# Per-head normalisation of queries and keys in block 2: one VectorE operation a head in place of a VectorE and a GpSimd pass

## The chip, the cores and the metric

The kernel runs on one core of a Trainium2 chip, with the engines TensorE, VectorE, ScalarE, GpSimd and the DMA queues beside one another. The metric is the device time of one execution in microseconds. Before the change it is 2656.02 us, the median of 3 runs (2654.87 to 2657.49).

## What is computed

Two transformer blocks behind one another on a sequence of 256 tokens and a width of 1024, each with two layers. The second, in which the change lies, carries 256 latent and 256 context tokens. In each of its layers one projection feeds a convolution branch, a neighbourhood attention and a grouped-query attention. The change touches how the last one's queries (8 heads) and keys (2 heads), 64 columns each, are normalised and rotated:

```python
def rmsnorm_2(x, g):
    xf = x.astype(jnp.float32)
    y = xf * lax.rsqrt(jnp.mean(xf * xf, axis=-1, keepdims=True) + EPS)
    return (y * g.astype(jnp.float32)).astype(x.dtype)

g_kc = rmsnorm_2(heads(gkc, GQA_KV_HEADS), k_norm_g[l])
q = axial_rope(rmsnorm_2(heads(gq, GQA_Q_HEADS), q_norm_g[l]), pos_row, pos_col)
k = axial_rope(rmsnorm_2(heads(gk, GQA_KV_HEADS), k_norm_g[l]), pos_row, pos_col)
cq = rmsnorm_2(heads(gqc, GQA_Q_HEADS), q_norm_g[l])
```

Latent tokens are normalised and rotated, context tokens only normalised. In the last layer the context has no queries of its own, only keys.

## The kernel before

Each engine has its own instruction stream, written out by hand, and they meet through semaphores. Block 2's projection stage is a row of items, each the products of one piece of weights (1024 rows by 256 columns) with the activations: four `glu` items (convolution branch), then `gkv`, `gq` (2), `nak` (2), `naq` (2) and `nav` (2), which are items 4 to 12. Products are done in three terms from an upper and a lower part of the float32 values: ScalarE copies the upper part of a piece (L1155), VectorE subtracts it and leaves the lower part (L773, `split2_low`), and TensorE takes both (L1913 with the activations as the moving side, L1948 with the weights moving). "Split n" below is L773 on piece n, and TensorE waits for it before item n. Item 11 is the first `nav` item, at L1948.

What VectorE does in this stage stands in the table `LEAD`, one list for each layer: numbers are taps of the depthwise convolution (L3235, 31 taps on 4 chunks, each 512 columns in layer 0 and 256 in layer 1), `(LOW, n)` is split n, `(SUMS, s)` and `(NORMS, 0)` belong to the normalisation. The stretch around the change is

```python
# layer 0
(SUMS, 3), 5, (LOW, 10), 7, (NORMS, 0), (LOW, 11), 8, (LOW, 12), 7, (LOW, 13), 9, (LOW, 14), 3
# layer 1
(SUMS, 3), 11, (LOW, 10), 11, (NORMS, 0), 2, (LOW, 11), 4, (LOW, 12), 12, (LOW, 13), 8, (LOW, 14)
```

The normalisation works on `gtok`, 128 tokens on the partitions by 4 token tiles `s` (0 and 1 latent, 2 and 3 context) by 640 columns (10 heads of 64; heads 8 and 9 are the keys). In profiles `gtok` lies in the buffer `G`, the factors `gss` in `small`, the rotation's temporaries in `A`. ScalarE squares (L1639), VectorE sums each head (L3255), ScalarE takes the root (L1664), VectorE the reciprocal (L3264), and in `g_norms` VectorE multiplies each tile by its factors, one operation for a tile (L3269), which counts `g_normed`.

GpSimd waits for `g_normed` of tile s. At s = 0 it first issues four DMAs that load two tables of the neighbourhood attention's bias (L1052). Then it multiplies the tile by the norm's weights, the 8 query heads (L1062) and the 2 key heads (L1065), and for the latent tiles it rotates: four products (L987), a difference (L989) and a sum (L990), which counts `roped_g`. Context tiles count it behind the multiplication. After the four tiles it adds the mask to the two tables (L1086). TensorE transposes `gtok` (L2440) when `roped_g` is complete, behind the projection's last item; then come the convolution branch's mean (L2432, which wants all taps) and the attention pairs (L2459, with the softmax's steps on VectorE L2876, L2880) woven with the products of the gates.

Of the kernel before, what the change touches and what calls it, by code (L numbers as in the profile page):

```python
# [16 lines left out]
ALU = mybir.AluOpType  # L17
# [3 lines left out]
P = 128  # L21
# [27 lines left out]
HD = 64  # L49
# [340 lines left out]
def program(nc, g, out):  # L390

    with ExitStack() as ctx:
# [29 lines left out]
        gain_qk = sb("gain_qk", DEPTH * 2 * HD)[:, :].rearrange("p (l k d) -> p l k d", l=DEPTH, k=2)  # L422
# [116 lines left out]
        gtok = G[:, 0:2560].rearrange("p (s n) -> p s n", s=4)  # L539
# [23 lines left out]
        gss = take(40).rearrange("p (s h) -> p s h", s=4)  # L563
# [22 lines left out]
        def pcol(name, i=0, layer=None, per=0):  # L586
# [54 lines left out]
        gsq_ready, gss_ready, groot_ready, g_normed, roped_g = (sem(n) for n in (  # L641
            "gsq_ready", "gss_ready", "groot_ready", "g_normed", "roped_g"))
# [291 lines left out]
        def _(pool):  # L934
# [57 lines left out]
            for l in range(DEPTH):  # L992
                chain = Chain(pool, pool_done, l * POOL_CHAIN1)
# [11 lines left out]
                for s in range(2):  # L1005
                    v = idxt[:, s, 0:576].rearrange("p (h d) -> p h d", h=9)
# [8 lines left out]
                for s in range(2):  # L1015
                    if s:
                        pool.wait_ge(roped_qk, (l * 2 + 1))
                    v = qkv[:, s, 0:2048].rearrange("p (h d) -> p h d", h=16)
# [14 lines left out]
            chain = Chain(pool, pool_done, (DEPTH * POOL_CHAIN1))  # L1033
            item, masked, bias_n, used = ITEM2, 0, 0, 0
            for layer in range(DEPTH):
                last = layer == DEPTH - 1
# [15 lines left out]
                        pool.dma_start(dst, src).then_inc(bias_landed[n % 2], 16)  # L1052

                for s in range(4):
                    h0 = 8 if last and s >= 2 else 0
                    pool.wait_ge(g_normed, 4 * layer + s + 1)
                    if s == 0:
                        load_bias(0)
                        load_bias(1)
                    v = gtok[:, s, :].rearrange("p (h d) -> p h d", h=10)  # L1060
                    if not h0:
                        chain(pool.tensor_tensor(v[:, 0:8, :], v[:, 0:8, :],  # L1062
                                                 gain_qk[:, layer, 0, :].unsqueeze(1).broadcast_to([P, 8, HD]),
                                                 ALU.mult))
                    ins = pool.tensor_tensor(v[:, 8:10, :], v[:, 8:10, :],  # L1065
                                             gain_qk[:, layer, 1, :].unsqueeze(1).broadcast_to([P, 2, HD]), ALU.mult)
                    if s >= 2:
                        ins.then_inc(roped_g, 1)
                        continue
                    chain(ins)  # L1070
                    chain.settle()
                    v = gtok[:, s, :].rearrange("p (h r e f) -> p h r e f", h=10, r=2, e=2)
                    cs_, sn_ = [t[:, s].unsqueeze(1).broadcast_to([P, 10, 2, 16]) for t in (cos2, sin2)]

                    pool.wait_ge(gss_ready, 4 * (layer + 1))
                    if s:
                        pool.wait_ge(roped_g, 4 * layer + 1)
                    rotate(v[:, :, :, 0, :], v[:, :, :, 1, :], cs_, sn_, [rope2[:, n] for n in range(4)], chain,
                           roped_g)
# [1437 lines left out]
        def _(dve):  # L2517
# [393 lines left out]
            for l in range(DEPTH):  # L2911
                items, poss, norm = l * ITEMS1, l * PIECES1, l * 3
                chain = Chain(dve, dve_done, (DVE_START) + l * DVE_CHAIN1)
# [90 lines left out]
                def head_rows(t):  # L3004
# [10 lines left out]
                                         op1=ALU.mult).then_inc(adt_ready, 1)  # L3015
# [11 lines left out]
                for u in range(8):  # L3027
                    s = u // 4
                    dve.wait_ge(relu_ready, (l * 8 + (u + 1)))
                    for e in range(2):  # L3030
                        h, n = 2 * (u % 4) + e, 2 * u + e
                        if h:
                            dve.wait_ge(score_step, (steps + n))
                        dve.scalar_tensor_tensor(out=score[s], in0=relu_buf[:, u % 2, T * e:T * e + KEYS[s]],
                                                 scalar=wi[:, s, h:h + 1],
                                                 in1=score[s] if h else caus[:, s, 0:KEYS[s]], op0=ALU.mult,
                                                 op1=ALU.add).then_inc(score_step, 1)
# [54 lines left out]
                for i in range(PAIRS + 2):  # L3092
                    if 1 <= i < PAIRS + 1:
                        c = i - 1
                        dve.wait_ge(decay_ready, done + c + 1)
                        for e in range(2):
                            h, half = 2 * c + e, mt[c % 2][:, e, :]
                            dve.scalar_tensor_tensor(out=half[:, 0:T], in0=half[:, 0:T], scalar=dt[:, 0, h:h + 1],
                                                     in1=cbm[:, h // 8, 0, :], op0=ALU.mult, op1=ALU.mult)
                            ins = dve.scalar_tensor_tensor(out=half[:, T:384], in0=half[:, T:384],  # L3100
                                                           scalar=dt[:, 1, h:h + 1], in1=cbm[:, h // 8, 1, 128:T],
                                                           op0=ALU.mult, op1=ALU.mult)
                        ins.then_inc(mt_ready, 1)
                    qkv_ahead("head", 2 * i - 1)
                    if i < PAIRS:
# [3 lines left out]
                        for e in range(2):  # L3109
                            h, half, row = 2 * i + e, mt[i % 2][:, e, :], M[(i + 1) % 2][:, T * e:T * (e + 1)]  # L3110
# [77 lines left out]
            for layer in range(DEPTH):  # L3188
# [70 lines left out]
                def g_norms():  # L3259

                    for s in range(4):
                        h0 = 8 if last and s >= 2 else 0
                        dve.wait_ge(groot_ready, 4 * layer + s + 1)
                        chain(dve.reciprocal(gss[:, s, h0:10], gss[:, s, h0:10]))  # L3264
                    chain.settle()
                    for s in range(4):
                        h0 = 8 if last and s >= 2 else 0
                        v = gtok[:, s, HD * h0:640].rearrange("p (h d) -> p h d", d=HD)
                        dve.tensor_tensor(v, v, gss[:, s, h0:10].unsqueeze(2).broadcast_to([P, 10 - h0, HD]), ALU.mult)\  # L3269
                           .then_inc(g_normed, 1)  # L3270

                n_issued = 0
                for n in range(4):
# [211 lines left out]
```

## Time and profile before

| | |
|---|---|
| median of 3 runs | 2656.02 us |
| the profiled execution | 2657.64 us, its span 2655.80 us |
| TensorE busy (products) | 2617.2 us, 99% |
| VectorE busy | 1928.6 us, 73% |
| ScalarE busy | 1278.2 us, 48% |
| GpSimd busy | 594.0 us, 22% |
| mean granted TensorE clock | 0.997 |

Shares of busy time are averages over stages. The stages of the change lie at 1380 to 1460 us (layer 0) and 2195 to 2270 us (layer 1). In the views, PE is TensorE, PEld its weight load, DVE VectorE, ACT ScalarE, POOL GpSimd; L12 is line 12 of the kernel.

### The profile page before, as it was taken

The numbers are of one execution on the slowest core, as the hardware profiler recorded it, in microseconds if no ns is written. First come the engines' busy times: TensorE is split into PE (matmuls) and PEld (weight loads), VectorE is DVE, ScalarE is ACT, GpSimd is POOL, SyncE is SP. The second block draws the span as 40 slices with busy tenths as digits, with TensorE's granted clock in tenths as the row PEclk, the third lists the DMA queues.
The fourth block names the chain that finished last, engine by engine and source line by source line (L and its number), as shares of the span: only waits on it lengthen the run. The fifth ranks groups of instructions, "written<-read, shape, count | busy, mean of one in ns | idle before, by whom it ended". The sixth has DMA issues, their size and how long they took to land.

```text
span 2655.8 us, 40458 instructions
## 1 busy us (share of the span) xinstructions
PE 2617.2 (99%) x17054; PEld 2285.5 (86%) x17054; DVE 1928.6 (73%) x2550; ACT 1278.2 (48%) x1659; POOL 594.0 (22%) x419
## 2 busy tenths in 40 slices
PE   8999999999999999999999999999999999999999
PEld 7889888888889987988898777778888899889887
DVE  7867576885876657687799655468778779865884
ACT  5445546544444545544523544544444443655543
POOL 3411010331330001132105301024303203411430
PEclk9999999999999999999999999999999999999999
DMA  7555795555555688455333322245555544434653
GB/s 245 186 192 179 245 301 165 185 186 194 190 181 177 206 269 270 159 190 194 91 96 100 85 70 64 70 142 192 188 186 191 181 120 129 122 116 147 219 182 103
DMA packets 442330, 445.57 MB, mean 168 GB/s; under 512 B 13711, under 2 KB 433672, under 8 KB 442150
## 3 DMA queue, kind: packets, MB, share of 16 engines
q1 hardware_dynamic: 438744, 436.80, 51.5%
q0 software_dynamic: 2400, 5.40, 1.0%
q8 instruction: 135, 2.21, 0.4%
q10 hardware_dynamic: 1006, 0.79, 0.1%
q14 instruction: 45, 0.37, 0.0%
HBM read 441.79 MB, written 1.17 MB: 167 GB/s over the span
## 4 chain that ended last, share of the span: by engine, by line
PE 90%; DVE 4%; issue 2%; ACT 2%; DMA 1%; POOL 1%; SPq 0%; ACTq 0%; DVEq 0%; POOLq 0%
PE bank L1953 31%; PE bank L1913 22%; PE bank L1957 16%; PE bank L1905 6%; PE bank L1948 4%; PE bank L2229 2%; PE bank L2468 1%; PE bank L2459 1%; PE bank L2139 1%; DVE lower L773 1%; DVE R L3235 1%; PE bank L2312 1%; DMA ring<-in_w_in 0%; PE bank L2326 0%; DMA bias_na<-rpb_scratch 0%
## 5 line engine op out<-in xcount | busy, mean ns | idle before, releaser
L1226 ACT ACTIVATE upper<-ring 128x2048 fp32r<-128x2048 f32 (+1 forms) x238 | 443.9, 1867 | 625.8 <-PE bank L1957 618.8
L2616 DVE TENSOR_TENSOR lower<-ring,upper 128x2048 fp32r<-128x2048 f32 (+1 forms) x238 | 596.0, 2505 | 190.2 <-ACT upper L1226 189.9
L1953 PE MATMUL bank<-h_pair,upper 128*128 128x512 f32 x2464 | 606.5, 393 | 10.8 <-DVE h_pair L2633 5.9
L1953 PEld LDWEIGHTS bank<-h_pair,upper 128*128 128x128 f32 x2464 | 455.8, 189 | 102.0 <-issue 11.7
L1957 PE MATMUL bank<-h_pair,lower 128*128 128x256 f32 x2464 | 339.7, 284 | 0.0
L1913 PE MATMUL bank<-h_up,lower 128*128 128x512 f32 (+1 forms) x1280 | 337.5, 346 | 0.7 <-DVE h_low L2683 0.7
L1957 PEld LDWEIGHTS bank<-h_pair,lower 128*128 128x128 f32 x2464 | 325.6, 192 | 11.4
L1953 PE MATMUL bank<-hid_pair,upper 128*128 128x512 f32 x1232 | 297.4, 392 | 0.0
L980 POOL TENSOR_TENSOR A<-A 128x512 f32<-128x512 f32 x77 | 209.4, 2719 | 334.5 <-ACT A L1275 334.5
L1913 PEld LDWEIGHTS bank<-h_up,lower 128*128 128x128 f32 x1280 | 223.6, 189 | 46.3 <-issue 17.3
L1953 PEld LDWEIGHTS bank<-hid_pair,upper 128*128 128x128 f32 x1232 | 225.7, 188 | 43.2
L773 DVE TENSOR_TENSOR lower<-ring,lower 128x2048 fp32r<-128x2048 f32 x70 | 164.9, 2356 | 99.9 <-ACT lower L1155 99.9
L766 DVE TENSOR_TENSOR lower<-ring,upper 128x2048 fp32r<-128x2048 f32 (+1 forms) x66 | 149.7, 2268 | 105.1 <-ACT upper L1147 105.1
L1913 PE MATMUL bank<-h_low,lower 128*128 128x512 f32 (+1 forms) x640 | 218.7, 342 | 0.0
L1155 ACT ACTIVATE lower<-ring 128x2048 fp32r<-128x2048 f32 x70 | 134.4, 1920 | 113.1 <-DMA ring<-in_w_in 82.5
L978 POOL TENSOR_TENSOR A<-A 128x512 f32<-128x512 f32 x77 | 121.3, 1575 | 277.6 <-DVE A L2724 146.5
L1905 PE MATMUL bank<-upper,h_pair 128*128 128x256 f32 x896 | 168.9, 290 | 0.0
L1957 PEld LDWEIGHTS bank<-hid_pair,lower 128*128 128x128 f32 x1232 | 159.8, 191 | 7.1
L1957 PE MATMUL bank<-hid_pair,lower 128*128 128x256 f32 x1232 | 162.0, 283 | 0.0
L3235 DVE SCALAR_TENSOR_TENSOR R<-R,params 128x512 f32<-128x512 f32 (+1 forms) x240 | 153.6, 706 | 0.5
L1905 PEld LDWEIGHTS bank<-upper,h_pair 128*128 128x128 f32 x896 | 140.5, 192 | 9.0 <-issue 7.7
L1147 ACT ACTIVATE upper<-ring 128x2048 fp32r<-128x2048 f32 (+1 forms) x66 | 124.2, 1881 | 46.9 <-PE bank L1913 28.0
(377 smaller groups left out, 4291.6 us busy)
## 6 DMA issues: line engine op xcount, KB each, us to landing
ring<-in_w_ffn_in SPq DMA_DIRECT2D x154, 1024.0 KB, 5.1
ring<-in_w_ffn_out SPq DMA_DIRECT2D x56, 1024.0 KB, 4.9
ring<-in_w_mix_in SPq DMA_DIRECT2D x48, 1024.0 KB, 5.4
ring<-in_w_mod SPq DMA_DIRECT2D x48, 1024.0 KB, 7.4
ring<-in_w_in SPq DMA_DIRECT2D x42, 1024.0 KB, 5.3
ring<-in_w_ffn_out SPq DMA_DIRECT2D x28, 768.0 KB, 4.2
ring<-in_w_mix_out SPq DMA_DIRECT2D x16, 1024.0 KB, 5.5
ring<-in_w_in SPq DMA_DIRECT2D x16, 512.0 KB, 4.6
```

The source lines that it names most:

```text
L766: eng.tensor_tensor(lowers[piece.slot][:, 0:w], slots[piece.slot][:, 0:w], uppers1[piece.up][:, 0:w].bitcast(F32), ALU.subtract).then_inc( ...
L773: eng.tensor_tensor(lowers[piece.slot], slots[piece.slot], uppers2[piece.up].bitcast(F32), ALU.subtract)\
L980: pool.tensor_tensor(buf, buf, r, ALU.mult).then_inc(glu_scaled, 1)
L1147: act.activation(uppers1[piece.up][:, 0:w], slots[piece.slot][:, 0:w], ACT.Copy).then_inc(up1_ready, 1)
L1155: act.activation(uppers2[piece.up], slots[piece.slot], ACT.Copy).then_inc(up2_ready, 1)
L1226: act.activation(f.upper(p)[:, 0:n], slot[:, 0:n], ACT.Copy).then_inc(up_ready, 1)
L1905: mm = pe.matmul(o, x_[:, k, tokens], w_[:, c], start=k == 0 and n == 0, stop=k == KD - 1 and n == 2)
L1913: mm = pe.matmul(out, w_[:, w_cols], x_, start=first and n == 0, stop=last and n == 2)
L1953: pe.matmul(bank[:, 0:2 * T], up[:, cols], x_pair.rearrange("p e t -> p (e t)"), start=first, stop=False)
L1957: return pe.matmul(bank[:, 0:T], low[:, cols], x_pair[:, 0, :], start=False, stop=last)
L2616: dve.tensor_tensor(f.lower(p)[:, 0:n], slot[:, 0:n], f.upper(p)[:, 0:n].bitcast(F32), ALU.subtract)\
L3235: ins = dve.scalar_tensor_tensor(out=dst, in0=src, scalar=w, in1=dst, op0=ALU.mult, op1=ALU.add)
```

## The change

VectorE's four multiplications by tile and GpSimd's multiplications by the weights are replaced by one scalar_tensor_tensor on VectorE for each head: the head's 64 columns times its factor (a column of `gss`, one value for each partition) times the weights `gain_qk`. That is 40 operations in layer 0 and 24 in layer 1 (10, 10, 2 and 2). `g_normed` is counted by the last head of a tile. GpSimd keeps the table DMAs, the rotation of the latent tiles and the masks; for context tiles it only passes the count on.

```diff
@@ -1052,23 +1052,13 @@
                         pool.dma_start(dst, src).then_inc(bias_landed[n % 2], 16)
 
                 for s in range(4):
-                    h0 = 8 if last and s >= 2 else 0
                     pool.wait_ge(g_normed, 4 * layer + s + 1)
                     if s == 0:
                         load_bias(0)
                         load_bias(1)
-                    v = gtok[:, s, :].rearrange("p (h d) -> p h d", h=10)
-                    if not h0:
-                        chain(pool.tensor_tensor(v[:, 0:8, :], v[:, 0:8, :],
-                                                 gain_qk[:, layer, 0, :].unsqueeze(1).broadcast_to([P, 8, HD]),
-                                                 ALU.mult))
-                    ins = pool.tensor_tensor(v[:, 8:10, :], v[:, 8:10, :],
-                                             gain_qk[:, layer, 1, :].unsqueeze(1).broadcast_to([P, 2, HD]), ALU.mult)
                     if s >= 2:
-                        ins.then_inc(roped_g, 1)
+                        pool.sem_inc(roped_g, 1)
                         continue
-                    chain(ins)
-                    chain.settle()
                     v = gtok[:, s, :].rearrange("p (h r e f) -> p h r e f", h=10, r=2, e=2)
                     cs_, sn_ = [t[:, s].unsqueeze(1).broadcast_to([P, 10, 2, 16]) for t in (cos2, sin2)]
 
@@ -3265,9 +3255,11 @@
                     chain.settle()
                     for s in range(4):
                         h0 = 8 if last and s >= 2 else 0
-                        v = gtok[:, s, HD * h0:640].rearrange("p (h d) -> p h d", d=HD)
-                        dve.tensor_tensor(v, v, gss[:, s, h0:10].unsqueeze(2).broadcast_to([P, 10 - h0, HD]), ALU.mult)\
-                           .then_inc(g_normed, 1)
+                        for h in range(h0, 10):
+                            v = gtok[:, s, HD * h:HD * (h + 1)]
+                            ins = dve.scalar_tensor_tensor(out=v, in0=v, scalar=gss[:, s, h:h + 1],
+                                                           in1=gain_qk[:, layer, h // 8, :], op0=ALU.mult, op1=ALU.mult)
+                        ins.then_inc(g_normed, 1)
 
                 n_issued = 0
                 for n in range(4):
```

## Rows read from the trace of the kernel before

**Rows 1.** the page: busy time by engine, and the chain by engine

```profile
PE 2617.2 (99%) x17054; PEld 2285.5 (86%) x17054; DVE 1928.6 (73%) x2550; ACT 1278.2 (48%) x1659; POOL 594.0 (22%) x419
...
PE 90%; DVE 4%; issue 2%; ACT 2%; DMA 1%; POOL 1%; SPq 0%; ACTq 0%; DVEq 0%; POOLq 0%
```

**Rows 2.** TensorE's waits (waiter <- releaser: total us, times, longest)

```profile
PE bank L1913 <- DVE R L3306: 2.5, 1, 2.5
PE bank L1948 <- DVE lower L773: 2.0, 1, 2.0
PE bank L1948 <- DVE R L2825: 1.7, 1, 1.7
...
PE bank L2440 <- ACT sq L1696: 0.6, 1, 0.6
```

**Rows 3.** the chain, layer 1 (start us, us, what)

```profile
2204.19 3.56 DVE R L3235 x9
...
2240.15 24.81 PE bank L1948 x192
...
2267.05 1.73 PE bank L2432 x8
```

**Rows 4.** windows (us: engines' busy time, PEclk the granted clock)

```profile
2228.50:2240.10 11.60, 9.67 (x81) 9.46 (x79) 11.57 (x24) 6.32 (x11) 3.83 (x5) 1.00 0.64 197
2240.10:2243.80 3.70, 3.65 (x18) 3.65 (x19) 3.70 (x4) 0.05 (x1) 3.53 (x4) 0.54 0.91 285
...
2178.00:2186.00 8.00, 6.33 (x54) 6.16 (x53) 7.37 (x15) 3.81 (x5) 0.00 (x0) 1.00 0.51 162
...
2318.50:2322.60 4.10, 3.88 (x20) 3.91 (x21) 3.23 (x9) 3.04 (x5) 1.26 (x2) 0.58 0.71 196
```

**Rows 5.** VectorE's groups from 2195 to 2236 us (busy us, mean ns)

```profile
L3235 DVE SCALAR_TENSOR_TENSOR R<-R,params 128x256 f32<-128x256 f32 x70 | 28.3, 478 | 0.0
```

**Rows 6.** timeline of VectorE, layer 1 (start us, us, what)

```profile
2235.13 1.97 DVE L3269 TENSOR_TENSOR G<-G,small 128x640 f32<-128x640 f32 x4
2237.01 0.88 DVE L3235 SCALAR_TENSOR_TENSOR R<-R,params 128x256 f32<-128x256 f32 x2
2237.81 2.29 DVE L773 TENSOR_TENSOR lower<-ring,lower 128x2048 fp32r<-128x2048 f32 x1
...
2244.09 2.97 DVE L773 TENSOR_TENSOR lower<-ring,lower 128x2048 fp32r<-128x2048 f32 x1
2246.98 11.93 DVE L3235 SCALAR_TENSOR_TENSOR R<-R,params 128x256 f32<-128x256 f32 x12
```

**Rows 7.** timeline of GpSimd, layer 1 ([idle before <- releaser])

```profile
2236.26 2.47 POOL L1052 DMA_DIRECT2D bias_na<-rpb_scratch  x4 [79.80 <-DVE G L3269]
...
2252.04 3.94 POOL L987 TENSOR_TENSOR A<-G,trig 128x320 f32<-128x320 f32 x4 [0.17 <-POOL G L1065]
...
2270.92 2.61 POOL L1052 DMA_DIRECT2D bias_na<-rpb_scratch  x4 [8.06 <-DVE A L2880]
```

**Rows 8.** timeline of VectorE in block 1, the nearest short operation

```profile
1029.75 0.34 DVE L3100 SCALAR_TENSOR_TENSOR A<-A,small,R 128x128 f32<-128x128 f32 x1
1030.01 0.48 DVE L3111 TENSOR_SCALAR A<-bank,small 128x256 f32<-128x256 f32 x1
```

**Rows 9.** timeline of VectorE, layer 0

```profile
1411.94 3.03 DVE L3269 TENSOR_TENSOR G<-G,small 128x640 f32<-128x640 f32 x4
1414.89 4.16 DVE L773 TENSOR_TENSOR lower<-ring,lower 128x2048 fp32r<-128x2048 f32 x1
```

**Rows 10.** the chain, layer 0

```profile
1428.83 23.03 PE bank L1948 x192
```

**Rows 11.** timeline of GpSimd, layer 0

```profile
1413.06 2.51 POOL L1052 DMA_DIRECT2D bias_na<-rpb_scratch  x4 [110.66 <-DVE G L3269]
1415.59 1.30 POOL L1062 TENSOR_TENSOR G<-G,gain_qk 128x512 f32<-128x512 f32 x1
```

**Rows 12.** timeline of VectorE in block 1, GpSimd rotating beside it

```profile
359.54 0.81 DVE L3100 SCALAR_TENSOR_TENSOR A<-A,small,R 128x128 f32<-128x128 f32 x1
```

## Prediction, made before the changed kernel was run

> **What bounds the kernel now.** I read the shares of the page first [rows 1]: TensorE is busy 99% of the span, and its products are 90% of the chain that ended last. So work added to VectorE, or taken off GpSimd, moves the end only where TensorE waits for one of them. The list of TensorE's waits [rows 2] has one such wait beside the change: 2.0 us at L1948 for `lower`, VectorE's output of L773. The chain through layer 1's projection stage [rows 3] shows its place: up to 2240 us it consists of VectorE's own instructions, and at 2240.15 TensorE resumes, right behind weight split 11. The normalisation of the queries and keys stands ahead of split 11 in VectorE's order, so every microsecond added to it is a microsecond for TensorE. In layer 0 the same order has room: split 11 is written at 1419.05 (1414.89 + 4.16) [rows 9] and its first product is due at 1428.83 [rows 10], 9.8 us later.
>
> The wait in layer 1 has a second price. The granted clock was 1.00 before it and 0.54 from 2240.1 to 2243.8 [rows 4], so TensorE ran there mostly at 1.2 GHz. The same 192 products took 24.81 us [rows 3] against 23.03 in layer 0 [rows 10]: 1.78 us.
>
> **VectorE and GpSimd at the same time.** A tap of 256 columns takes 0.478 us with GpSimd idle [rows 5]. Twelve taps behind one another took 11.93 us while GpSimd multiplied [rows 6], about 1.02 each, with one GpSimd product of 128x320 to each tap (four of them took 3.94 us from 2252.04) [rows 7]. A tap's columns are 256/0.96 = 0.27 us of this, so a GpSimd product holds VectorE off for 0.75; I take 0.76. The two engines take turns, one instruction each, however long either is: an operation of 128 columns took 0.81 us beside GpSimd [rows 12] and 0.34 alone [rows 8]. What counts is how many VectorE instructions are still to come when GpSimd begins.
>
> **The change, part by part.**
>
> *VectorE's four multiplications* (L3269) go. In layer 1 they took 1.88 us from the first start to the next instruction (2235.13 to 2237.01) [rows 6], in layer 0 2.95 us (1411.94 to 1414.89) [rows 9].
>
> *VectorE's per-head operations* come: 10+10+2+2 = 24 in layer 1, 40 in layer 0, each on 64 columns with a per-partition factor. The trace has none so short of this form. The nearest row is the form on 128 columns, whose successor starts 0.26 us later (1029.75 to 1030.01) [rows 8]; 64 columns less, at one per 1/0.96 ns, take off 0.067: 0.196 us. From below: the four TENSOR_TENSORs of 640 columns repeat every 0.74 us [rows 9], 0.07 over their columns, so 0.134 is the least for 64. From above, without overlap of neighbours, 0.28. I take 0.196, the value of the same form: 24 x 0.196 = 4.70 us in layer 1 (3.2 to 6.7), 40 x 0.196 = 7.84 in layer 0.
>
> The Trainium skill ("VectorE: DVE Perf Modes", the TRN2 errata section) speaks against this change: VectorE pays a fixed cost per instruction, so many small tiles pay it each time, and its figure from SBUF is 58 cycles plus the columns. By that, an estimate, 64 columns take 122 cycles, 0.127 us. The direction is that of the rows; the size is not, since for 128 columns the figure gives 0.19 where the row has 0.26.
>
> *GpSimd's 14 gain multiplications* (L1062, L1065) go. Its order becomes: four table DMAs, two rotations of six products each, then the mask additions. The table DMAs took VectorE no time in layer 1: its taps beside them began 0.40 us apart [rows 6, 7].
>
> *Layer 1, split 11.* The tenth operation ends at 2235.13 + 9 x 0.196 + 0.28 = 2237.17. GpSimd's first DMA follows 0.3 us behind (before, 2235.13 + 0.83 to 2236.26), the four take 2.47, and the first product comes 0.17 later for its semaphores [rows 7]: 2240.1. VectorE is through its 24 operations at 2239.83, so the first of the two taps goes ahead, to 2240.30. Then they take turns: GpSimd to 2241.06, second tap (0.27) to 2241.33, GpSimd to 2242.09, split 11 (2048 columns, 2.13) to 2244.2. Before, it was 2240.10. **Plus 4.1 us**: 2.8 of instructions, 1.3 of turns that GpSimd took behind the split before.
>
> *Layer 0, split 11.* GpSimd starts rotating at 1411.94 + 1.76 + 0.28 + 0.3 + 2.51 + 0.17 = 1416.95 [rows 9, 11]; 25 of the 40 operations are issued by then. Beside operations of 64 columns its twelve products come every 0.76 + 0.07 = 0.83 us: 10.0 us and some 0.5 of gaps between its groups, to 1427.5. VectorE gets one operation into each turn and one into each gap, 15 in all, so its 40th ends at 1427.5 too. Split 11 takes 2.2 more: 1429.8. TensorE wants it at 1428.83. **Plus 1.0 us**; of the 9.8 us of cover nothing is left. Bounds: nothing (at 0.134 the operations are done at 1417.3) and 2.5 us (two more turns).
>
> *What follows.* Layer 1: TensorE reaches the products of split 12 half of 24.8 us after 2244.2, at 2256.6; that split was ready at 2247.06 and is now some 4 us later [rows 6]. The taps' end hardly moves, since the turns of 14 multiplications are gone by then, and stays ahead of the mean's products at 2267.05 + 4 [rows 3]. Layer 0: eight taps of 0.66 (512/0.96 + 0.13), two mask additions and split 12 end at 1438.5, wanted at 1440.3. So the time freed on GpSimd pays VectorE back, but behind the instruction that TensorE waits for. An earlier rotation buys nothing: the transposes L2440 waited 0.6 us for ScalarE, not for GpSimd [rows 2].
>
> *The clock.* The low stretch of layer 1 stays (bounds: 1.78 us given back, if it falls where TensorE idles, and 1.78 more). The waits of 2.0 and 2.5 us were each followed by one, the 1.7 at L1948 was not (granted clock 1.00 from 2178 to 2186) [rows 2, 4]; the 1.0 of layer 0 should be without. The three runs spread by 2.6 us, one and a half such stretches, so some runs may escape the present one; with 6 us of wait none should. I add 0.3.
>
> **Sum.** 4.1 + 1.0 + 0.3 = 5.4 us. The profiled run took 2657.64 (span 2655.80), 1.6 above the median; the addition is the same for either: 2656.02 + 5.4 = 2661.4 us.
>
> **The rivals.**
> - *Forecast*, chance 0.50: both stages lose. 2661.4, own range 2660.0 to 2663.5.
> - *GpSimd gets in first*, 0.18. Split 11 of layer 0 took 4.16 us, 1.87 over its 2.29 [rows 6, 9], and was held from about 1415.0 although GpSimd's product was only issued at 1415.59 [rows 11]. If a rotation likewise holds VectorE during the last DMA of layer 1, each VectorE instruction caught behind it costs 0.8: three +2.5. About 2663.5. Against: the rotation stands behind a semaphore wait, that multiplication did not.
> - *Layer 0 stays covered*, 0.12: VectorE slips two short operations into a turn. The 40 are done by 1424, split 11 before 1428.83. Only layer 1 pays: 2660.4. Against: the 128-column operation, one to a turn [rows 12].
> - *Short operations cost 0.134*, 0.06: layer 0 nothing; in layer 1 they end at 2238.35, the split is issued at 2239.15, ahead of GpSimd's product, and ends at 2241.35. +1.25 and the 0.3: 2657.6. The skill's figure from the errata section leads to the same case.
> - *The low stretch falls into the wait*, 0.07: 1.78 back, 2659.6.
> - *The other side, no loss*, 0.07: GpSimd, free some 5 us earlier, shortens layer 1's pair stage, so that the 2.5 us wait at L3306 and the low stretch behind it (0.58) [rows 2, 4] go: 5.4 less 4.3, 2657.1. It decides if GpSimd is what that stage waits for. Against: it stood idle 8.06 us for VectorE before its next table DMA [rows 7].
>
> **How the numbers follow.** The range reaches from 2658.3 (layer 1 alone, its low stretch given back) to 2666.5 (three instructions caught, a second low stretch, some of layer 0's upper bound). 0.2% (5.3 us) is about what a measurement here can tell from none, and the forecast lies on that bound. Slower takes 0.6 of the forecast's chance, all of the second case and a little of the others: 0.50. Within 0.2%: 0.47. Faster, by a low stretch fewer elsewhere: 0.03.
>
> **What would show it.** Per-head operations 0.196 us apart while GpSimd is idle, 0.83 while it rotates. TensorE's wait at L1948 for L773 twice: 6 us in layer 1, 1 in layer 0. The taps of 2246 to 2262 with fewer at 1.02 us and more at 0.4, their end in place. GpSimd's busy time down by some 20 us. The prediction falls if layer 0 shows no wait, if split 11 of layer 1 ends before 2243, or if a low stretch comes or goes elsewhere.

## The result, and the profile after

The changed kernel takes 2667.14 us, the median of 4 runs (2665.52 to 2668.56), against 2655.44 for the kernel before in 4 runs beside it: ratio 1.0044, 95% interval 1.0032 to 1.0056, all of it above 0.2%. That is 11.7 us more where 5.4 were forecast, and 0.6 us above the upper end of the range. The profiled run took 2667.55 us with a span of 2665.7, 9.9 more than the span of before; the profiled run of the kernel before lies 2.2 us above the median of its four runs and this one 0.4, which is the rest of the 11.7.

The lines of the changed kernel lie 9 or 10 lower: the taps are L3225, the per-head operations L3260, the item with the weights moving is L1938 (before L1948), the first with the activations moving L1903 (before L1913), the masks are L1076. L773, L987, L989, L990 and L1052 are as before.

The page of the changed kernel, busy time by engine and the chain by engine:

```profile
PE 2618.6 (98%) x17054; PEld 2286.7 (86%) x17054; DVE 1932.6 (72%) x2606; ACT 1278.5 (48%) x1659; POOL 572.9 (21%) x405
...
PE 85%; DVE 9%; issue 2%; ACT 2%; DMA 1%; POOL 0%; SPq 0%; ACTq 0%; POOLq 0%
```

Against [rows 1], GpSimd works 21.1 us less and VectorE only 4.0 us more in the sum, yet VectorE's share of the chain went from 4% to 9%. The list of TensorE's waits (total us, times, longest) says where:

```profile
PE bank L1938 <- DVE lower L773: 12.3, 2, 9.4
```

Against the single wait of 2.0 us in [rows 2] there are now two, 2.95 us in layer 0 and 9.37 in layer 1. The chain of the changed kernel shows both (start us, us, what), first layer 1, then layer 0:

```profile
2233.42 4.36 DVE R L3225 x11
...
2238.10 9.37 DVE G L3260 x24
2247.47 0.79 DVE R L3225 x2
2248.26 2.21 DVE lower L773
...
2250.52 19.59 PE bank L1938 x148
```

```profile
1424.40 5.15 DVE G L3260 x12
1429.55 2.21 DVE lower L773
...
1431.80 13.26 PE bank L1938 x97
```

Between the reciprocals and split 11 there are now 9.30 us of per-head operations (2238.10 to 2247.40) in place of 1.88 [rows 6], and in layer 0 they are on the chain too.

The starts of TensorE's 17054 products, set against those of before one by one, give the account of the time. In layer 0 they are 3.1 us late behind the wait and 4.5 to 5.0 us late shortly after it, since the granted clock falls there. At 2181 us 1.5 us come back: the 1.67 us wait that stands there before [rows 2] is 0.3 in this run. In layer 1 another 7.4 are lost (10.4 late), at 2310 us 0.7 come back, and the end is 9.9 us late. So nearly all of it lies at the two waits. The windows of the changed kernel around them (us: busy time, then the granted clock):

```profile
1425.00:1431.50 6.50, 3.86 (x18) 2.85 (x16) 6.50 (x13) 1.33 (x3) 4.79 (x5) 1.00 0.17 49
1431.50:1434.90 3.40, 3.10 (x14) 3.10 (x15) 3.40 (x5) 0.66 (x1) 1.98 (x2) 0.50 0.61 214
...
2243.90:2254.00 10.10, 3.48 (x16) 3.48 (x17) 10.10 (x11) 1.91 (x1) 9.79 (x8) 0.50 0.30 92
```

TensorE worked at 1.2 GHz (granted clock 0.50) for 3.4 us behind the new wait of layer 0. In layer 1 the low stretch is longer than before [rows 4], but for the most part it lies in the wait itself: TensorE is busy for 3.48 us of it.

The ledger of VectorE in layer 1 closes to a few hundredths. Single operations on its timeline (start us, us):

```profile
2241.83 0.97 DVE L3260 SCALAR_TENSOR_TENSOR G<-G,small,gain_qk 128x64 f32<-128x64 f32 x1
2242.72 2.81 DVE L3260 SCALAR_TENSOR_TENSOR G<-G,small,gain_qk 128x64 f32<-128x64 f32 x1
2245.45 0.95 DVE L3260 SCALAR_TENSOR_TENSOR G<-G,small,gain_qk 128x64 f32<-128x64 f32 x1
2246.33 0.27 DVE L3260 SCALAR_TENSOR_TENSOR G<-G,small,gain_qk 128x64 f32<-128x64 f32 x1
2246.52 0.95 DVE L3260 SCALAR_TENSOR_TENSOR G<-G,small,gain_qk 128x64 f32<-128x64 f32 x1
```

and GpSimd's timeline beside them:

```profile
2240.45 2.47 POOL L1052 DMA_DIRECT2D bias_na<-rpb_scratch  x4 [79.51 <-DVE G L3260]
2242.93 0.88 POOL L987 TENSOR_TENSOR A<-G,trig 128x320 f32<-128x320 f32 x1
2243.75 0.87 POOL L987 TENSOR_TENSOR A<-G,trig 128x320 f32<-128x320 f32 x1
2244.57 0.86 POOL L987 TENSOR_TENSOR A<-G,trig 128x320 f32<-128x320 f32 x1
2245.40 0.92 POOL L987 TENSOR_TENSOR A<-G,trig 128x320 f32<-128x320 f32 x1
2246.40 0.99 POOL L989 TENSOR_TENSOR G<-A 128x320 f32<-128x320 f32 x1
2247.36 3.83 POOL L990 TENSOR_TENSOR G<-A 128x320 f32<-128x320 f32 x1
```

An operation beside an idle GpSimd lasts 0.28 us, and the next one starts 0.196 later. Twenty of the 24 are such. The operation of 2241.83 is held by 0.69 us while the third and fourth table DMA are issued. The one of 2242.72 is held by 2.53 us, through three of GpSimd's products, which follow one another without a gap. Two more are held by 0.67 us each, one product apiece. Together: 24 x 0.196 + 0.69 + 2.53 + 0.67 + 0.67 = 9.26 of the 9.30 us. Then it turns round: two taps and split 11 run unhindered (0.87 and 2.28 us) while GpSimd's sum of 2247.36 stands for 3.83 us. The wait follows: 2.0 as before, plus 4.70 - 1.88 = 2.8 for the longer instructions, plus 4.6 for the four holds, is 9.4.

In layer 0 the same two holds stand at the same place, 0.69 us at 1415.71 and 2.61 us at 1416.62 (an operation of 2.89), and nine operations behind them are held by one product each (0.97 to 0.99 us in place of 0.28). That is 7.84 + 0.69 + 2.61 + 9 x 0.70 = 17.4 of the 17.49 us from 1411.98 to 1429.47.

### The profile page after: what moved, and what is told of

Read it like the earlier page. It is cut to its first block, busy times and chain, and to the rows that moved or that the text cites. A ratio compares the mean times of both kernels' runs of the same rounds, so it can differ in the third digit from the quotient of the medians.

```text
span 2665.7 us, 40503 instructions
## 1 busy us (share of the span) xinstructions
PE 2618.6 (98%) x17054; PEld 2286.7 (86%) x17054; DVE 1932.6 (72%) x2606; ACT 1278.5 (48%) x1659; POOL 572.9 (21%) x405
## 4 chain that ended last, share of the span: by engine, by line
PE 85%; DVE 9%; issue 2%; ACT 2%; DMA 1%; POOL 0%; SPq 0%; ACTq 0%; POOLq 0%
PE bank L1943 31%; PE bank L1903 20%; PE bank L1947 16%; PE bank L1895 6%; DVE R L3225 3%; PE bank L1938 2%; DVE lower L773 2%; PE bank L2219 2%; PE bank L2458 1%; PE bank L2449 1%; PE bank L2129 1%; DVE G L3260 1%; PE bank L2302 1%; ACT lower L1145 1%; PE bank L2316 0%
## 5 line engine op out<-in xcount | busy, mean ns | idle before, releaser
L1903 PE MATMUL bank<-h_up,lower 128*128 128x512 f32 (+1 forms) x1280 | 337.4, 346 | 0.7 <-DVE h_low L2673 0.7
L1903 PEld LDWEIGHTS bank<-h_up,lower 128*128 128x128 f32 x1280 | 223.6, 189 | 46.2 <-issue 17.3
L773 DVE TENSOR_TENSOR lower<-ring,lower 128x2048 fp32r<-128x2048 f32 x70 | 163.8, 2340 | 101.1 <-ACT lower L1145 101.1
L1903 PE MATMUL bank<-h_low,lower 128*128 128x512 f32 (+1 forms) x640 | 218.7, 342 | 0.0
L3225 DVE SCALAR_TENSOR_TENSOR R<-R,params 128x512 f32<-128x512 f32 (+1 forms) x240 | 136.9, 642 | 0.5
```

The lines of the kernel that those rows point to most:

```text
L773: eng.tensor_tensor(lowers[piece.slot], slots[piece.slot], uppers2[piece.up].bitcast(F32), ALU.subtract)\
L1903: mm = pe.matmul(out, w_[:, w_cols], x_, start=first and n == 0, stop=last and n == 2)
L3225: ins = dve.scalar_tensor_tensor(out=dst, in0=src, scalar=w, in1=dst, op0=ALU.mult, op1=ALU.add)
```

## The experiments

Two theories stood after the comparison. By the first, *the holds beside GpSimd* make the loss: ahead of split 11 stand many short VectorE instructions, GpSimd's products hold them for some 0.7 us each, and the products right behind the table DMAs get in early and for three in a row. By the rival, the loss is the *number and duration of the instructions* themselves, or comes from what the change does on GpSimd, the rotation moved forward and the time freed.

**All tiles first.** GpSimd issues its table DMAs and then waits for all four tiles, so that no product stands beside a per-head operation.

```diff
 # GpSimd, changed kernel
                     if s == 0:
                         load_bias(0)
                         load_bias(1)
+                        pool.wait_ge(g_normed, 4 * layer + 4)
```

> The changed kernel, but GpSimd, after its four table DMAs, waits for all four tiles before it rotates the first. Theory 'holds' (the per-head operations cost 0.196 us as in the changed kernel's first ten; the rest of their 9.30 and 17.49 us was GpSimd's rotation holding the shared interface, from its last DMAs on): 24 operations in 4.7 us and 40 in 7.9, no TensorE wait at item 11 of layer 0, in layer 1 a wait of 5.5 to 7.5 us, since the two taps and split 11 now meet the rotation. About 2661. Theory 'the DMAs themselves hold it': operations beside the third and fourth DMA still take 0.7 us or more longer. Theory 'short operations slow down in a row': 9 and 17 us as in the changed kernel, and its 2667.

Measured: 2658.55 us (10 runs) against 2655.26 (25 runs), ratio 1.0012 (1.0003 to 1.0021). VectorE's timeline of this kernel, layer 0 and then layer 1, and GpSimd's in layer 1:

```profile
1411.28 7.95 DVE L3261 SCALAR_TENSOR_TENSOR G<-G,small,gain_qk 128x64 f32<-128x64 f32 x40
...
2233.08 4.79 DVE L3261 SCALAR_TENSOR_TENSOR G<-G,small,gain_qk 128x64 f32<-128x64 f32 x24
2237.78 0.87 DVE L3226 SCALAR_TENSOR_TENSOR R<-R,params 128x256 f32<-128x256 f32 x2
2238.57 2.28 DVE L773 TENSOR_TENSOR lower<-ring,lower 128x2048 fp32r<-128x2048 f32 x1
```

```profile
2235.42 2.47 POOL L1052 DMA_DIRECT2D bias_na<-rpb_scratch  x4 [81.08 <-DVE G L3261]
2237.94 6.70 POOL L987 TENSOR_TENSOR A<-G,trig 128x320 f32<-128x320 f32 x4
```

With this wait the kernel is 3.3 us above the kernel before, and without it 11.7, each against its own runs of the kernel before: it takes back 8.4 us. The operations take 4.70 and 7.85 us, the predicted 0.196 each. Layer 0 has no wait any more, and the one in layer 1 is 4.7: the old 2.0 and the 2.8 of instructions. So the holds, with the low clock behind them, cost some 8.4 us and the instructions themselves the rest. The time expected was 2661 and the wait in layer 1 5.5 to 7.5 us, because the two taps and split 11 were to meet the rotation. They met it and weren't held: they took 0.87 and 2.28 us, and it was GpSimd's first product that lasted through all three (3.64 us of the 6.70 for four). The last two table DMAs (to 2237.89) stand beside the last operations here and hold nothing, where in the changed kernel one was held by 0.69 us. What differs is the product behind them, which must wait for the other tiles here and was ready there.

**The wait in layer 0 only**, to see whether the two layers add up.

```diff
                         load_bias(1)
+                        if layer == 0:
+                            pool.wait_ge(g_normed, 4 * layer + 4)
```

> The changed kernel with the wait for all four tiles in layer 0 only. By the account of the trace layer 0 costs 3.1 us of wait and 1.4 of low clock, layer 1 7.4: the wait at item 11 of layer 0 goes, and the time is 4.5 us under the changed kernel's 2667.1: 2662.6. If the losses were not additive (the later state of the ring of weights gives some back), 2664 to 2667.

Measured: 2663.36 us (5 runs) against 2655.33 (14 runs), ratio 1.0033 (1.0020 to 1.0046). Against the changed kernel's 2667.14 layer 0 gives back 3.8 us, where the trace had 4.5; the run with both waits gives back 4.8 more for layer 1, where the trace had 4.6 of holds. The wait in layer 1 is 9.6 us in this kernel and 9.4 without any edit, so layer 1's loss doesn't hang on layer 0's. No run has the wait in layer 1 alone.

**Only VectorE's part.** GpSimd keeps its 14 multiplications, so the weights are applied twice.

```diff
 # the kernel before, VectorE alone changed
-                        dve.tensor_tensor(v, v, gss[:, s, h0:10]... , ALU.mult).then_inc(g_normed, 1)
+                        for h in range(h0, 10):
+                            ins = dve.scalar_tensor_tensor(out=v, in0=v, scalar=gss[:, s, h:h + 1],
+                                                           in1=gain_qk[:, layer, h // 8, :], ...)
+                        ins.then_inc(g_normed, 1)
```

> Only VectorE's part of the change: per-head operations by factor and weights, while GpSimd keeps its 14 gain multiplications (the weights are thus applied twice). Theory: the loss sits in the operations caught beside GpSimd's products right behind its table DMAs, whatever these products are; wait in layer 1 9 us, in layer 0 3 us or more, since there are eight products more and the one of 512 columns is longer: 2667 to 2670. Rival, that it is the rotations moved forward that hold VectorE: without them 5 us less, 2660 to 2662.

Measured: 2672.52 us (4 runs) against 2655.33 (14 runs), ratio 1.0067 (1.0051 to 1.0084), 17.2 us more. TensorE's waits and VectorE's timeline, layer 0 and layer 1:

```profile
PE bank L1948 <- DVE lower L773: 15.4, 2, 8.7
```

```profile
1411.46 21.26 DVE L3270 SCALAR_TENSOR_TENSOR G<-G,small,gain_qk 128x64 f32<-128x64 f32 x40
...
2244.35 8.61 DVE L3270 SCALAR_TENSOR_TENSOR G<-G,small,gain_qk 128x64 f32<-128x64 f32 x24
2252.88 0.87 DVE L3235 SCALAR_TENSOR_TENSOR R<-R,params 128x256 f32<-128x256 f32 x2
```

The direction was foreseen, the size was not: 2.5 us above the end of what was expected, and it is layer 0, where the wait is 6.6 us and not 3. There GpSimd has 16 products for its first two tiles and four more for the others, and VectorE's 40 operations last (to 1432.7) until those 16 are over. In layer 1 the 24 operations take 8.6 us with a gain multiplication behind the table DMAs as they take 9.3 with a rotation there. So it isn't the rotation moved forward that holds VectorE, and that part of the rival is out. Its other part, the duration of the instructions, is the 3.3 us that the run with the wait for all tiles still costs.

**Only GpSimd's part.** Its 14 multiplications are left out, VectorE keeps its four; the weights are applied nowhere.

```diff
 # the kernel before, GpSimd alone changed
-                    if not h0:
-                        chain(pool.tensor_tensor(v[:, 0:8, :], ... gain_qk[:, layer, 0, :] ...))
-                    ins = pool.tensor_tensor(v[:, 8:10, :], ... gain_qk[:, layer, 1, :] ...)
                     if s >= 2:
-                        ins.then_inc(roped_g, 1)
+                        pool.sem_inc(roped_g, 1)
                         continue
```

> Only GpSimd's part of the change: its 14 gain multiplications are left out, VectorE keeps its four multiplications by the factors (the weights of queries and keys are thus applied nowhere). Theory: what was lost comes from VectorE's many instructions ahead of split 11; with four of them as before, split 11 begins ahead of GpSimd's first rotation product in layer 1 and the 2.0 us wait stays as it is, layer 0 keeps its cover: 2655 us, as the kernel before, within 1. Rival: the products that stand right behind the table DMAs hold VectorE wherever they are, and with rotations in place of gain multiplications there the wait grows: 2657 to 2659. If the freed time of GpSimd is worth something, 2653 or less.

Measured: 2654.36 us (10 runs) against 2655.33 (14 runs), ratio 1.0000 (0.9991 to 1.0010). TensorE's wait, and VectorE's and GpSimd's timeline in layer 1:

```profile
PE bank L1939 <- DVE lower L773: 1.9, 1, 1.9
```

```profile
2235.05 1.96 DVE L3260 TENSOR_TENSOR G<-G,small 128x640 f32<-128x640 f32 x4
2236.93 0.88 DVE L3226 SCALAR_TENSOR_TENSOR R<-R,params 128x256 f32<-128x256 f32 x2
2237.72 2.28 DVE L773 TENSOR_TENSOR lower<-ring,lower 128x2048 fp32r<-128x2048 f32 x1
```

```profile
2238.65 5.14 POOL L987 TENSOR_TENSOR A<-G,trig 128x320 f32<-128x320 f32 x4
```

GpSimd is busy for 16.5 us less (577.5 in place of 594.0), and this is worth nothing that can be measured here, because with four instructions in place of 24 split 11 has begun at 2237.72, ahead of the first product (2238.65), which then waits for it. Beside many VectorE instructions the same saving is worth 5.4 us (2672.5 to 2667.1). The two parts of the change don't add: 17.2 and nothing make 11.7.

**Table DMAs behind the rotations.** The issue of the four DMAs is moved behind the loop over the tiles, so that the rotation begins without them.

```diff
                 for s in range(4):
                     pool.wait_ge(g_normed, 4 * layer + s + 1)
-                    if s == 0:
-                        load_bias(0)
-                        load_bias(1)
 ...
+                load_bias(0)
+                load_bias(1)
                 for n in range(NA_UNITS):
```

> The changed kernel with the first four table DMAs behind both rotations instead of ahead of them. Theory 'a product that stands behind DMAs takes the interface early and keeps it': the two long holds of the changed kernel (0.98 and 2.81 us for one short operation) are gone, every operation beside the rotation takes 0.9 to 1.0 us, one a product; but the rotation starts 2.5 us earlier and meets 14 operations of layer 1 instead of 5, so the 24 take 12 to 14 us and the layer 1 wait grows to 12 us or more: 2669 to 2671. Theory 'any first product of a rotation holds it for 2.5 us': the long hold appears again at the rotation's start. Rival 'the DMAs are what costs': 24 operations in about 6 us, 2662.

Measured: 2667.02 us (4 runs) against 2655.26 (25 runs), ratio 1.0048 (1.0031 to 1.0064), no different from the changed kernel. One operation of VectorE, and GpSimd's timeline, in layer 1:

```profile
2236.32 0.98 DVE L3259 SCALAR_TENSOR_TENSOR G<-G,small,gain_qk 128x64 f32<-128x64 f32 x1
```

```profile
2236.29 3.59 POOL L987 TENSOR_TENSOR A<-G,trig 128x320 f32<-128x320 f32 x4 [79.33 <-DVE G L3259]
2239.95 0.99 POOL L989 TENSOR_TENSOR G<-A 128x320 f32<-128x320 f32 x1
```

The long hold is gone: here every operation that meets a product lasts 0.95 to 0.98 us, one to a product. But the rotation begins with the first tile's operations just done, and nine operations are caught in place of four: 4.70 + 9 x 0.70 = 11.0 us, against 9.3. So the hold of three products needs products that stand right behind the DMAs, and without it this layer pays no less, because more of the operations meet GpSimd: its wait is 10.7 us and was 9.4. In layer 0 it is 1.7 in place of 2.95, and the two nearly cancel. More had been expected, 14 operations caught and 2669 to 2671 us.

**Whole tiles on VectorE.** One operation of 640 columns by the factors, then one of 512 and one of 128 by the weights: 10 operations in layer 1 and 12 in layer 0.

```diff
-                        for h in range(h0, 10):
-                            ins = dve.scalar_tensor_tensor(...64 columns...)
+                        chain(dve.tensor_tensor(v, v, gss[:, s, h0:10].unsqueeze(2)..., ALU.mult))
+                        for a, b, k in ((0, 8, 0), (8, 10, 1)):
+                            ins = dve.tensor_tensor(v[:, a:b, :], v[:, a:b, :], gain_qk[:, layer, k, :]..., ALU.mult)
```

> The changed kernel, but VectorE multiplies a whole tile by its factors (one operation of 640 columns) and then by the weights in two (512 and 128 columns), 10 operations in layer 1 and 12 in layer 0 instead of 24 and 40; GpSimd as in the changed kernel. Theory 'number of instructions that GpSimd catches': the ten take about 4 us in layer 1, since GpSimd's hold falls on the taps and the split behind them, the twelve about 10 us in layer 0, where no wait remains; in layer 1 a wait of 5.5 to 8 us: about 2661. Theory 'columns count': the same multiplications take 1.3 times the columns of the per-head form, and the time stays at 2667.

Measured: 2659.93 us (10 runs) against 2655.26 (25 runs), ratio 1.0019 (1.0009 to 1.0028). Two rows of VectorE in layer 1:

```profile
2239.13 1.09 DVE L3225 SCALAR_TENSOR_TENSOR R<-R,params 128x256 f32<-128x256 f32 x1
2240.14 2.95 DVE L773 TENSOR_TENSOR lower<-ring,lower 128x2048 fp32r<-128x2048 f32 x1
```

The same multiplications with under half of the instructions cost 4.7 us in place of 11.7. They take 3.9 us in layer 1 and are over before GpSimd's first product; two instructions are still held, a tap by 0.6 us during the DMAs and split 11 by 0.7, and the wait is 5.1. Layer 0 has none. This run changes two things at once, the number of instructions and the time until they are done, and it doesn't tell one from the other.

**The normalisation later.** In VectorE's order it goes behind split 11 in layer 0 and behind split 12 in layer 1, everything else as in the changed kernel.

```diff
-          (LOW, 10), 7, (NORMS, 0), (LOW, 11), 8, (LOW, 12), ...
+          (LOW, 10), 7, (LOW, 11), (NORMS, 0), 8, (LOW, 12), ...
-          (LOW, 10), 11, (NORMS, 0), 2, (LOW, 11), 4, (LOW, 12), 12, (LOW, 13), 8, (LOW, 14)
+          (LOW, 10), 11, 2, (LOW, 11), 4, (LOW, 12), (NORMS, 0), 12, (LOW, 13), 8, (LOW, 14)
```

> The changed kernel with the normalisation moved in VectorE's order: in layer 0 from ahead of split 11 to behind it, in layer 1 behind split 12. Theory 'only what stands ahead of split 11 costs': no TensorE wait at item 11 in either layer, the low-clock stretches there gone, against the kernel before 2.0 and 1.8 us less: about 2651.6. Per-head operations as slow as in the changed kernel, but covered. Rival 'VectorE as a whole is short of time in this stage': a wait of several us appears at item 12, at the mean or at the transposes, and the time is 2656 or more.

Measured: 2659.42 us (10 runs) against 2655.26 (25 runs), ratio 1.0018 (1.0009 to 1.0028); 2651.6 had been expected. The waits of item 11 are gone as foreseen, but TensorE waits elsewhere. Its waits, then VectorE and GpSimd in layer 1:

```profile
PE bank L2430 <- POOL G L990: 4.1, 1, 4.1
...
PE bank L1938 <- DVE lower L773: 1.8, 1, 1.8
```

```profile
2251.98 4.83 DVE L3225 SCALAR_TENSOR_TENSOR R<-R,params 128x256 f32<-128x256 f32 x12
2256.73 2.28 DVE L773 TENSOR_TENSOR lower<-ring,lower 128x2048 fp32r<-128x2048 f32 x1
```

```profile
2251.94 7.81 POOL L990 TENSOR_TENSOR G<-A 128x320 f32<-128x320 f32 x1
```

What was overlooked is that GpSimd can be held for long as well: one sum lasted 7.81 us, through twelve taps and a split that all ran at the speed they have alone. The second rotation came that much later, and the transposes of the queries waited 4.1 us for it, with a low stretch of the clock behind. In layer 0 split 12 was late by 1.8 us.

**A version that takes both into account.** In layer 1 the normalisation stands between splits 11 and 12, and split 13 stands behind all taps, right ahead of split 14; GpSimd waits for all four tiles. The order alone was also given to the kernel before, and the order with the wait to the version with whole tiles.

```diff
-          (LOW, 10), 11, (NORMS, 0), 2, (LOW, 11), 4, (LOW, 12), 12, (LOW, 13), 8, (LOW, 14)
+          (LOW, 10), 11, 2, (LOW, 11), (NORMS, 0), 4, (LOW, 12), 12, 8, (LOW, 13), (LOW, 14)
```

> The kernel before with one change of order in VectorE's layer 1: the normalisation stands behind split 11 and its two taps, and the taps ahead of splits 12 and 13 are rearranged (split 13 stands behind the last taps but one group). If the 2.0 us wait of the kernel before at split 11 comes only from the normalisation standing ahead of it, wait and low clock stretch there go: 3.8 us less. The rival is that GpSimd, which begins later and still has its 14 gain multiplications, is complete only at some 2266 us, behind the transposes that are due about 2262, and the wait returns there with 4 to 5 us. By the first about 2651.5 us, by the second 2654 to 2658.

> The changed kernel, with GpSimd waiting for all four tiles before it rotates, and the same order of VectorE's layer 1 as in the run above. Theory: per-head operations that stand beside no GpSimd product cost 0.196 us each and, behind split 11, are covered by TensorE's products: item 11 without a wait (3.8 us less than the kernel before), rotations complete at about 2260, ahead of the transposes, since 14 multiplications are gone. About 2652 us. Rival: GpSimd is shut out by the taps, as in the run with the later normalisation (one product took 7.8 us there), and the transposes wait 4 us: 2656 to 2658.

> As the run above, but VectorE multiplies whole tiles: one operation by the factors, then one of 512 and one of 128 columns by the weights, in place of ten per-head operations. By the durations measured these take 3.9 us in layer 1 in place of 4.7, off the path in either form: 2651 to 2652, the same as the run above within what can be measured. If the two differ by over 2 us, the number of VectorE's instructions beside GpSimd counts even here.

Measured, against 2654.37 us for the kernel before (27 runs): before with the order 2653.44 (11 runs, ratio 0.9995, 0.9987 to 1.0004), changed kernel with wait and order 2651.87 (11 runs, 0.9989, 0.9980 to 0.9998), whole tiles with wait and order 2652.09 (11 runs, 0.9993, 0.9985 to 1.0002). In the second the wait at item 11 is gone and nothing longer than 0.5 us takes its place; VectorE and GpSimd in layer 1:

```profile
2235.60 2.28 DVE L773 TENSOR_TENSOR lower<-ring,lower 128x2048 fp32r<-128x2048 f32 x1
...
2238.20 4.79 DVE L3261 SCALAR_TENSOR_TENSOR G<-G,small,gain_qk 128x64 f32<-128x64 f32 x24
2242.91 1.67 DVE L3226 SCALAR_TENSOR_TENSOR R<-R,params 128x256 f32<-128x256 f32 x4
```

```profile
2258.80 1.79 POOL L1077 TENSOR_TENSOR bias_na<-bias_na,namask 128x256 f32<-128x256 f32 x2
```

The rotations are complete at 2258.8, ahead of the transposes. This version is the only one whose interval lies below the kernel before, by 0.02% at least; how much of its 2.5 us is the order and how much the change stays open, since the kernel before with that order alone (1.1 us of wait left, at the mean, L2432) is 0.9 us under the kernel before and the two intervals overlap. For the kernel before with the order alone neither expectation held: the wait of 2.0 us at item 11 went, yet 0.9 us came back and not 3.8, and the 4 to 5 us of wait feared for it did not come: with split 13 out of the way its GpSimd was through with the rotations and multiplications at 2260.8. The 0.8 us that whole tiles save VectorE cannot be seen once they are off the path.

## Why the prediction was wrong

The price of an instruction was right. The per-head operations start 0.196 us apart wherever GpSimd is idle, as worked out from the 128-column row [rows 8]; the bounds of 0.134 and 0.28 were not needed. The Trainium skill's figure ("VectorE: DVE Perf Modes", the TRN2 errata section, 58 cycles plus the columns) had given an estimate of 0.127, a third less than measured, and with it the rival *short operations cost 0.134* fell. Right too were the start of GpSimd's first product (the tenth operation ends at 2240.15, the four DMAs begin at 2240.45 and the product at 2242.93, the predicted 0.3 and 2.47 us behind one another; only the 0.17 us for semaphores is missing), the 2.8 us of instructions in layer 1, the existence of both waits, GpSimd's busy time (21.1 us down), and that the cover of 9.8 us in layer 0 is used up.

The step that failed is the sentence that "the two engines take turns, one instruction each, however long either is", and with it the one that "the table DMAs took VectorE no time in layer 1". That second sentence rests on two taps, which started at 2237.01 and 2237.41, beside the first two DMAs; beside the third and fourth stood only split 11 [rows 6, 7]. The forecast of layer 1 had 1.3 us of turns, all behind the 24 operations, at the taps and the split. In its place came 0.69 us during the last two DMAs and 2.53 us for three products without a turn for VectorE, which put off the last operations so that two more were caught at 0.67 each; behind them, where the forecast had its 1.3, nothing was lost at all. So the term was 4.6 and not 1.3, and layer 1 cost 7.4 and not 4.1. The rival *GpSimd gets in first* had the first half of this, down to its row (split 11 of layer 0 held from 1415.0, while the last DMA was still being issued [rows 9, 11]), and not the three products in a row. It had the chance of 0.18 and a price of 2.5 us, 2.1 in its time, where 3.3 were due. The reason given against it, that the rotation stands behind a semaphore wait, did not apply: the wait of 0.17 us in [rows 7] is for the gain multiplication, which the change takes out, and the first product follows the last DMA at once.

Layer 0 was forecast at 1.0 us of wait and came out at 2.95. By the forecast 25 operations were through before GpSimd began, and 15 met one product or gap each. In the run 19 were through when the hold of the last DMA began, and the twelve products held ten operations, since three of them held the same one; seven were left when the rotation was over (1428.09), and ran to 1429.47. The bound of 2.5 us above, "two more turns", was passed by half a microsecond, and with a wait of 2.95 us the granted clock fell behind it, some 1.4 to 1.6 us that had been left out on the ground that a wait of 1.7 us was without such a stretch.

The step on the clock in layer 1 held (the stretch stays and costs as before). That the time freed on GpSimd pays back only behind the instruction that TensorE waits for is right for the taps: twelve of them took 7.05 us in place of 11.93 [rows 6],

```profile
2257.41 7.05 DVE L3225 SCALAR_TENSOR_TENSOR R<-R,params 128x256 f32<-128x256 f32 x12
```

and GpSimd's part alone is worth nothing. It is not the whole of it, though. Beside the 40 operations of layer 0 the shorter work of GpSimd is worth a good deal ahead of split 11: the wait there is 2.95 us with it and 6.6 without. The other side, a gain from GpSimd being free earlier, did not come: TensorE's wait for `R` behind the pairs is 2.6 us after and was 2.5 [rows 2].

The sum by its terms, in the profiled runs: layer 1 +7.4 (forecast 4.1), layer 0 +3.1 (1.0), clock +1.4 to 1.6 (0.3), and 2.2 given back in two places that no step of the prediction spoke of, at 2181 and 2310 us. The first is a wait that stands in nearly every run of this study and was missing in the profile of the changed kernel; it was not followed further.

## What to carry to other kernels

Where VectorE and GpSimd both read on-chip memory, count VectorE's instructions between the moment at which GpSimd can start and the next thing that TensorE waits for: each may cost 0.7 us there beside a GpSimd product of 320 columns, whatever its own size, so 24 operations of 64 columns cost more than 4, or 10, that do the same work. Where work does move from GpSimd to VectorE, look at GpSimd's start too: one wait that let VectorE finish first gave back 8.4 of 11.7 us here, though that kernel was still 0.12% slower than the one before. And when an order is changed, look at both directions, since GpSimd's own short instruction can stand for a whole group of VectorE's, and what comes behind it may be the next thing that is late.

## What the runs showed of the hardware

The Trainium skill ("SBUF — State Buffer", section "SBUF: two separate sides") says that VectorE and GpSimd contend for one pair of ports as an exclusive lock, held for the whole of an instruction by whichever starts first, for a VectorE operation with two inputs in SBUF beside a GpSimd operation that reads it. The traces agree with the exclusion: a short operation lasted 0.28 us alone and 0.95 to 0.98 beside one product, whose own time stayed at 0.86 to 0.99. What the rule leaves open is who goes next, and there three things were not expected.

- *GpSimd three in a row.* In both layers of the changed kernel a VectorE operation of 64 columns lasted 2.8 to 2.9 us while three products ran, always the first products behind the table DMAs; so it was in both layers with the normalisation later and in layer 1 with the wait in layer 0 only. With the DMAs moved behind the rotations it was not seen, nor with a gain multiplication as the first product (one operation of 2.45 us, through the last DMAs and that one product), nor where taps or whole tiles stood beside the first products.
- *VectorE for a whole group.* A sum of GpSimd lasted 3.83 us in the changed kernel, through two taps and a split, and 7.81 with the normalisation moved, through twelve taps and a split; with turns it has 0.9 to 1.1. Both began just as VectorE went from the per-head operations to the taps, and ended 0.7 us behind the next split. A product did the same at that place with the DMAs moved (3.84 us) and in VectorE's part alone (3.85), and so did the first product of the rotation in the run with the wait for all tiles (3.64). Behind the split the two engines took turns.
- *A hold ahead of the product.* During the third and fourth table DMA a VectorE operation or a tap was held by 0.6 to 0.7 us (0.97 for 0.28, 1.09 for 0.47), in both layers of the changed kernel and in layer 1 with whole tiles. In each of these a product stood ready behind the DMAs; with the wait for all tiles, where none was ready, operations beside the same DMAs kept their 0.196. The version with whole tiles, wait and order has that wait too, but VectorE's last tile was done at 2240.10, before the DMAs were through, and the second tap behind it was held:

```profile
2240.42 1.10 DVE L3226 SCALAR_TENSOR_TENSOR R<-R,params 128x256 f32<-128x256 f32 x1
```

That fits a product that takes the ports before the profile shows its start, but it was not tried by itself, and a ready product doesn't always get in. In the kernel before split 11 of layer 1 started beside the third DMA and ran its 2.29 us [rows 6, 7], and in layer 0 with whole tiles VectorE's operations and split 11 went on at full speed while the first product waited for them:

```profile
1416.93 4.01 POOL L987 TENSOR_TENSOR A<-G,trig 128x320 f32<-128x320 f32 x1
```

Which rule hands the ports from one engine to the other was not found; these are regularities of this kernel's traces, and no run changed the arbitration by itself.
